# Mixing stage of a fused two-block kernel: the two heads of an attention pair laid down in turn in the two halves of the array

## What is computed

```python
# neighbourhood attention, 8 heads of 64: each query sees a window of 256 keys and 256 context keys
s_win = einsum('bcqhd,bkcjhd->bhcqkj', q_r, kb) * scale + bias      # masked outside the window
s_ctx = einsum('bcqhd,blhd->bhcql', q_r, k_ctx) * scale
p = softmax(concatenate([s_win, s_ctx], -1))
o = einsum(p_win, vb) + einsum(p_ctx, v_ctx)
# HGRN2, 4 heads of 128, forward and backward: S_t = diag(f_t) S_{t-1} + k_t^T v_t, o_t = q_t S_t
```

## Time and profile before

| | |
|---|---|
| time, median of 3 executions | 2451.6 us (2449.45 to 2453.14) |
| the profiled execution: its own time | 2451.39 us |
| its span in the profile | 2449.6 us |
| mixing stage in it | from 291.9 us to 537.7 us, where the next stage's first product starts |
| TensorE clock granted, mean | 0.973 of full speed |

### The profile page before, as it was taken

The page is one execution under the profiler, slowest core; times in us unless marked ns, Lnnn a source line. Parts: engine busy times, 40 slices in busy tenths (PEclk is TensorE's granted clock), DMA queues, the critical chain, the costliest instruction groups (busy, mean ns, idle before and its releaser), DMA issues. The chain is left out here.

```text
span 2449.6 us, 32335 instructions
## 1 busy us (share of the span) xinstructions
PE 2250.8 (92%) x12803; PEld 2017.8 (82%) x12803; DVE 1780.1 (73%) x2985; ACT 924.3 (38%) x1210; POOL 629.7 (26%) x357
## 2 busy tenths in 40 slices
PE   5999887978998999999999899999999897889997
PEld 3888676756898999899999899999999676677775
DVE  7555687763689999999995687788786657754543
ACT  4222233333232333455553233333333534566332
POOL 0000232311346776533224433333331000000000
PEclk8999998989999999999999999999999999999999
DMA  6567400011236777688889999999996222111221
GB/s 250 206 239 243 146 8 1 1 69 52 94 111 224 238 243 250 248 309 342 322 332 367 361 350 354 361 348 353 359 351 215 79 78 86 44 52 61 78 86 69
DMA packets 178103, 488.73 MB, mean 200 GB/s; under 512 B 13696, under 2 KB 80384, under 8 KB 166432
## 3 DMA queue, kind: packets, MB, share of 16 engines
q1 hardware_dynamic: 141088, 352.43, 41.6%
q0 software_dynamic: 36864, 134.23, 14.2%
HBM read 432.08 MB, written 52.43 MB: 198 GB/s over the span
## 5 line engine op out<-in xcount | busy, mean ns | idle before, releaser
L1066 PE MATMUL ps<-h_high,u_high 128*128 128x384 f32 (+1 forms) x1216 | 430.8, 354 | 43.4 <-POOL u_low L1256 19.1
L1067 PE MATMUL ps<-h_low,u_high 128*128 128x384 f32 (+1 forms) x1216 | 421.4, 347 | 0.0
L1068 PE MATMUL ps<-h_high,u_low 128*128 128x384 f32 (+1 forms) x1216 | 421.2, 346 | 0.0
L1066 PE MATMUL ps<-w_high,v_high 128*128 128x384 f32 x1024 | 344.5, 336 | 10.0 <-DVE w_low L1636 10.0
L1067 PE MATMUL ps<-w_low,v_high 128*128 128x384 f32 x1024 | 343.5, 335 | 0.0
L1068 PE MATMUL ps<-w_high,v_low 128*128 128x384 f32 x1024 | 343.4, 335 | 0.0
L1066 PEld LDWEIGHTS ps<-h_high,u_high 128*128 128x128 f32 x1216 | 231.0, 190 | 58.7 <-POOL u_low L1256 22.1
L1393 ACT ACTIVATE v_high<-v_raw 128x2048 fp32r<-128x2048 f32 x64 | 122.6, 1916 | 346.8 <-PE ps L1068 346.8
L1066 PE MATMUL ps<-h_high,w_high 128*128 128x512 f32 x560 | 227.7, 407 | 25.6 <-DVE h_low L2289 10.3
L1067 PEld LDWEIGHTS ps<-h_low,u_high 128*128 128x128 f32 x1216 | 231.4, 190 | 8.3 <-issue 1.2
L1068 PEld LDWEIGHTS ps<-h_high,u_low 128*128 128x128 f32 x1216 | 231.0, 190 | 8.0
(11 more groups left out here) (428 smaller groups left out, 4436.8 us busy)
## 6 DMA issues: line engine op xcount, KB each, us to landing
v_raw<-in_peer_v SPq DMA_DIRECT2D x64, 1024.0 KB, 6.8
w_raw<-in_w SPq DMA_DIRECT2D x99, 512.0 KB, 3.7
u_first<-in_uT SPq DMA_DIRECT2D x32, 1024.0 KB, 6.5
u_second<-in_uT SPq DMA_DIRECT2D x32, 1024.0 KB, 6.7
xT<-in_late_w SPq DMA_DIRECT2D x56, 512.0 KB, 4.4
gelu_up<-gelu SPq DMA_DIRECT2D x128, 192.0 KB, 7.2
gates<-gates_sb SPq DMA_DIRECT2D x12, 2048.0 KB, 12.9
weighted<-gelu_up SPq DMA_DIRECT2D x64, 384.0 KB, 6.9
```

Of the source, the lines that this page charges most:

```text
L1066: pe.matmul(out, wh, mh, start=start, stop=False)
L1067: pe.matmul(out, wh, ml, start=False, stop=False)
L1068: return pe.matmul(out, wl, mh, start=False, stop=stop)
```

## The change

The scores of both heads of a pair are issued together in the even slot, window of head one, window of head two, context of head one, context of head two; the value products of both heads likewise, alternating head by head, and in the even slot two after the odd item's. values now stands ahead of turn in the slot. VectorE waits for the scores of both heads, and does the odd item first in its slot, ahead of that slot's recurrence steps.

```diff
 # TensorE
-            def scores(i):
+            def scores_of_pair(i):
                 if i >= 2:
-                    pe.wait_ge(maxed, 2 * (i - 1))
+                    pe.wait_ge(maxed, 2 * i)
...
+                rows = [slice(0, DH), slice(DH, P)]
+                for s, a in enumerate(rows):
+                    win = k.kT[a, hp, 0:T].rearrange("p (r x) -> p r x", r=ROWS)[:, :, k0:k0 + KB]
+                    pe.matmul(ps[:, s, 0:WIN], k.qT[a, hp, c * P:(c + 1) * P], win, start=True, stop=True)
+                for s, a in enumerate(rows):
+                    pe.matmul(ps[:, s, WIN:512], k.qT[a, hp, c * P:(c + 1) * P], k.kT[a, hp, T:T + C], start=True,
+                              stop=True).then_inc(scored, 1)
...
-            def values(i):
+            def values_of_pair(i):
+                first_head, c = items[i]
+                pe.wait_ge(turned_sb, i + 2)
+                if i:
+                    pe.wait_ge(stored, i // 2)
                 for j in range(4):
+                    v = k.vw[:, 2 * c + j, :] if j < 2 else k.vc[:, j - 2, :]
+                    for s in range(2):
+                        h = first_head + s
+                        last = pe.matmul(ps[DH * s:DH * (s + 1), 3, 0:P], v[:, h * DH:(h + 1) * DH],
+                                         pT[:, s, j * P:(j + 1) * P], start=j == 0, stop=j == 3)
+                        if j == 3:
+                            last.then_inc(summed, 1)
...
             for n in range(SLOTS_N):
-                if n < N:
-                    scores(n)
+                if n < N and n % 2 == 0:
+                    scores_of_pair(n)
                 for kind, x, s in fill[n]:
...
+                if 0 <= n - 4 < N and n % 2 == 0:
+                    values_of_pair(n - 4)
                 if 0 <= n - 2 < N:
                     turn(n - 2)
-                if 0 <= n - 3 < N:
-                    values(n - 3)
 # ScalarE, copy of the transposes
-                        act.wait_ge(summed, i - 1)
+                        act.wait_ge(summed, 2 * (i // 2))
 # VectorE
-                dve.wait_ge(scored, n + 1)
+                dve.wait_ge(scored, 2 * (n // 2) + 2)
                 if n >= 3:
                     dve.wait_ge(turned, n - 2)
...
             for n in range(SLOTS_N):
+                if n < N and n % 2:
+                    item(n)
                 for kind, x, s in fill[n]:
...
-                if n < N:
+                if n < N and n % 2 == 0:
                     item(n)
                 if 0 <= n - 1 < N:
                     inverse(n - 1)
```

More of the change, by code:

```diff
@@ L690, in _ @@
         def _(pe):
-            def scores(i):
-                h, c = items[i]
-                a, hp = DH * (h % 2), h // 2
+            def scores_of_pair(i):
+                hp, c = items[i][0] // 2, items[i][1]
                 if i >= 2:
-                    pe.wait_ge(maxed, 2 * (i - 1))
-                q = k.qT[a:a + DH, hp, c * P:(c + 1) * P]
+                    pe.wait_ge(maxed, 2 * i)
                 k0 = min(max(QB * c - KB // 4, 0), GW - KB)
[L698 to L701, removed]
+                rows = [slice(0, DH), slice(DH, P)]
[5 more added lines that the diff above has]
+                              stop=True).then_inc(scored, 1)
             def turn(i):
@@ L709, in turn @@
                 last.then_inc(turned, 1)
-            def values(i):
[L712 to L717, removed]
-                for j in range(4):
[L719 to L722, removed]
+            def values_of_pair(i):
[3 more added lines that the diff above has]
+                    pe.wait_ge(stored, i // 2)
+                for j in range(4):
+                    v = k.vw[:, 2 * c + j, :] if j < 2 else k.vc[:, j - 2, :]
[5 more added lines that the diff above has]
+                            last.then_inc(summed, 1)
             def context(d):
```

## The result

The changed kernel takes 2500.12 us (median of 4, 2498.27 to 2500.74) where the kernel before takes 2450.98 on the same chip: ratio 1.0195, 95% interval 1.018 to 1.0209, about 49 us or 2.0% slower. The prediction was 2507, range 2484 to 2524. The sign, the place and the wait that costs were right. Two terms were mis-sized in opposite directions: the overlap of the two halves was put at half of what it is, and the steps around the wait were put too short. That 2507 came within 7 us is in part luck.

A forecast was written before the change was run, and what follows sets the result against it. In the mixing stage neither TensorE nor VectorE filled the time; they ran in step. 2451.4 + 48.5 (waits and steps) + 19.9 (clock) - 12.5 (overlap) = 2507.3, say 2507 us; range 2484 to 2524, forecast band 2500 to 2514.

The forecast's parts named there:

- The sign: Whole kernel: the change was forecast to make it slower, chance 0.94.
- the wait that costs: Mixing stage, VectorE: the odd item waits for turn(n-2) before overwriting its s_sb buffer, about thirteen times, 3 us each.
- The stall: Mixing stage: VectorE and TensorE work in turn; eleven pairs lose 3.7 us each, +40.7 of the +48.5 us.
- The step between the levels: Even slot's level to the odd one's: 8.2 us without overlap, 7.9 in part, 7.2 in full, where it was 4.49.
- The clock: TensorE after twelve new 3.8 us pauses: level runs at half clock, 1.66 us each, +19.9 us, bounds 0 and +27.
- The overlap: Products of a pair's two array halves in scores and values: partial overlap saves 12.5 us, bounds 0 and 25.9.
- full overlap: Rival: a pair's scores and values cost one head's, -25.9; 2494 us with the clock's fall; chance 0.19, shared with clock staying up.
- hidden wait: Rival: item n+1's wait is hidden and the engines stay in step, 2445 us; chance 0.06.
- the 0.95 at the first level: Start of the mixing stage: item 1 no longer stands before the first qd, -0.95 us.
- 2.1 of 3.3 us: Odd item's wait: TensorE ends the turn 3.3 us after VectorE ends item n; full overlap takes 2.1 of it.
- A faster TensorE alone: Mixing stage before the change: with both engines in step, speeding up only TensorE is worth little.

The follow-up runs named there:

- x1: Changed kernel with four buffers of s_sb in place of three, item n waiting for turn(n-3): 2446.33 us, ratio 0.9974 to the kernel before.
- x2: Changed kernel with the odd item back behind its slot's recurrence steps on VectorE, three buffers: 2448.34 us, ratio 0.9987 to the kernel before.
- x4: Changed kernel with four unread products behind turn(n-2) in even slots, filling TensorE's pause: 2482.31 us, ratio 1.0113 to the kernel before.
- x3: Changed kernel with all products of a pair's first head listed before the second's, same slots and waits: 2508.14 us, ratio 1.0227 to the kernel before.
- x7: Changed kernel with four buffers of s_sb and the odd item back behind its slot's recurrence steps: 2443.79 us, ratio 0.9964 to the kernel before.

## Why the prediction was right, and where it was off

**The stall.** "The two engines now work in turn where they worked side by side": shown, by the waits after, and by x1 and x2. x1 loosens that one wait and keeps all else of the change; x2 puts the odd item back and keeps all that the change did on TensorE. The predicted 3.8 us pause twelve times is 3.98 us twelve times. The step between the levels was put at 8.2 us without overlap and 7.2 with all of it; it is 7.64 with all of it. Half of the gap of 0.4 is the copy: I took 0.65 us, half of a pair of copies, where the product starts 0.87 behind the first copy's start (396.40 to 397.27). The level ahead of 64-column products takes 1.98 and not 1.88 (389.63 to 391.61), and from turn's start to the item are 0.84 and not 0.74: 0.1 each.

**The clock.** +19.9 predicted from two pauses of the trace before; x4 gives 18.6 by medians with the wait left in place, 20.1 by the ratios, and 14.4 by the length of the stage in the two profiled executions (296.5 and 282.2 us). The level runs between 2.6 and 3.8 us behind these pauses, not always at half speed from its first record to its last, but turn and scores share the loss. The prediction's reading, that pauses over 3 us end at half speed and one of 2.21 did not, chose among the rows. Two more of the same trace don't fit a rule by length:

```profile
297.02 2.05 PE L735 MATMUL ps<-ic,qd 128*128 128x128 f32 x16 [2.98 <-ACT qd L869]
...
309.38 3.42 PE L759 MATMUL ps<-qd,kd 128*128 128x128 f32 x16 [2.18 <-DVE A_diag L927]
```

Behind 2.98 us the sixteen records ran at full speed, and behind 2.18 they did not; the granted clock from 309.3 to 312.8 was 0.57. "Both pauses over 3 us" leaves out a third, of 7.66 us ahead of 420.71, which ended at half speed too (3.78).

**The overlap** is the term that was mis-sized. The prediction took 12.5 us by the nearest row ("eight starts take five steps", and weight loads of 1.64 us), and gave full overlap the bound of 25.9. The values' sixteen weight loads fit into 1.02 us, so the sum of recorded load times of one half was no limit on two. The Trainium skill's rule ("TensorE: Matmul & The Clock Gate", Part 3), that products in different row groups run at once, holds here for float32 too, and for column halves (1.06 and 1.02 us for a pair). The same section says that matmuls start strictly in the order of the list; x3's records differ (head two's first starts at 396.15, head one's last ones at 396.25 and later), and here the measurement decides.

With full overlap the sum would have been 2494, which is the rival "full overlap" with the fall of the clock: of the mechanisms on record that one is what happened in the array, and the measured 2500.1 lies where its band and the forecast's meet. The stage grew by 50.9 us where that sum has 42.5, so 8.4 are missing. The starts in the two traces show three sizes: the twelve steps at 0.43 more, as above (+5.2); no gain at the first level, which came at 310.43 in place of 309.38, since the clock fell in the context steps this time (+2); and the last read-out, which starts 6.3 us behind the start of level 9 where it had started 3.4 behind it, since level 9 took 3.75 us at half speed in place of 1.97 (+2.9). They make 10.1, and the clock behind the twelve pauses, at 14 to 20 for 19.9, takes back up to 5.5. How the rest divides was not settled. The stages behind were 2.7 us shorter, as said. So the forecast's nearness to 2500 comes of 13 us too little for the overlap against some 8 too little for the steps.

**The other side.** The rival "hidden wait" (2445) is what x1 and x7 measure once the wait is truly gone: 2446 and 2444. Its place was right. Its price came out, but not term by term: the 0.95 at the first level is not there (level 1 comes 18.6 us behind the stage's first product in x1, 17.5 before). The reason to rule it out was right too, but its margin was misread. The prediction lets full overlap take 2.1 of 3.3 us; the scores' part moves VectorE's readiness as well as the turn, so only the values' 1.02 count. The turn ends 2.5 us after VectorE is ready for the odd item, even with full overlap.

**A faster TensorE alone.** "Worth little" holds as well: halving the time of scores and values takes 16 x (1.06 + 1.02) = 33 us of TensorE's work out of the stage, and at best 9 us come back (x7's 8.8), since VectorE then bounds the levels.

## What to carry to other kernels

When work of two iterations is drawn together on one engine, go through the buffer waits of the next engine in its new order: a wait that was always satisfied can become the one on the chain, and everything queued behind it moves too. Here the cure was one more buffer, or leaving the consumer's order alone. Pauses on TensorE are dearer than their length, since the work behind them may run at half the clock; if they can't be avoided, work moved into them (turn before values) pays twice.

## What the runs showed of the hardware

- Float32 products with 64 contraction partitions each, one in the lower and one in the upper half, run fully side by side: 1.07 us for a pair (x4, 384.77 to 385.84) where one head took 1.06; so do products into the lower and the upper 64 output partitions of one bank, 1.02 us for sixteen records.
- TensorE lets a free half overtake: in x3 records of the second head start ahead of three records of the first that stand earlier in the list (396.15 against 396.25 and later), in the scores as in the values.
- Behind a TensorE pause of 3.98 us the sixteen records of a level took 2.6 to 3.8 us, behind pauses of 2.96 us sometimes 2.02 and sometimes 3.75. In the kernel before it took 3.42 behind a pause of 2.18, and sixteen records took 2.05 behind one of 2.98, so the length of the pause alone does not tell.
